# RWKV half of a hybrid layer: the score branch's output taken out of its own visit and put into the fourth level of the triangular inverse

## The reference

```python
p = x @ w_in
o_sb = stick_breaking_attention(q, k, v)      # 8 heads of 128
o_rw, _ = rwkv7_group(p[..., 3072:], ...)     # 16 heads of 64
h = concatenate([o_sb, o_rw], axis=-1) @ w_out

# score branch, for each head
z = einsum('qd,sd->qs', q, k) * d ** -0.5
log_a = z + lax.cumsum(where(mask, log_sigmoid(-z), 0), reverse=True)
o_sb = exp(where(mask, log_a, -inf)) @ v

# RWKV branch, for each head and token
S = S * w_t - (S @ kk_t) (kk_t * a_t)^T + v_t k_t^T
y_t = S @ r_t
```

## Time and profile before

| | |
|---|---|
| median of three runs | 3052.69 us (3048.38 to 3052.90) |
| the profiled execution, its own time | 3052.2 us |
| its span | 3050.5 us |
| PE busy | 2962.2 us, 97% |
| DVE busy | 1798.3 us, 59% |
| ACT busy | 1453.9 us, 48% |
| mean DMA rate | 161 GB/s |
| chain that ended last, PE's share | 91% |
| the seven narrow groups with a mixer, period | 59.5 us each (L512 at 85.50, 145.04, ... 442.69) |

### The profile page before, as it was taken

One profiled execution on the slowest core, in us unless ns is written; L12 is line 12 of the kernel. 1 busy time (PEld: TensorE's weight loads), 2 busy tenths in 40 slices (PEclk: granted clock), 3 DMA queues, 4 the chain that ended last, 5 costly groups with the idle time before them and its releaser, 6 DMA issues.

```text
span 3050.5 us, 55918 instructions
## 1 busy us (share of the span) xinstructions
PE 2962.2 (97%) x22084; PEld 2607.1 (85%) x22084; DVE 1798.3 (59%) x2375; ACT 1453.9 (48%) x2241; POOL 13.1 (0%) x28
## 2 busy tenths in 40 slices
PE   8999999999999999999999999999999999999997
PEld 8888887778888888889999997999977888888886
DVE  4655565575554555564666665566667545555555
ACT  4544544344343444434566664456654434444342
POOL 0000000000000000000000000000000000000000
PEclk9999999999999999999999999999999999999999
DMA  7333334455555555544334433544335555555553
GB/s 228 110 111 106 108 115 138 166 191 192 190 188 192 187 193 188 190 160 138 120 135 142 137 128 136 182 140 139 132 121 219 191 192 186 194 190 192 188 187 111
DMA packets 156999, 491.86 MB, mean 161 GB/s; under 512 B 15584, under 2 KB 50528, under 8 KB 155776
## 3 DMA queue, kind: packets, MB, share of 16 engines
q1 hardware_dynamic: 154032, 476.18, 45.9%
q0 software_dynamic: 2224, 11.69, 1.0%
q10 hardware_dynamic: 544, 1.05, 0.1%
HBM read 486.76 MB, written 2.10 MB: 160 GB/s over the span
## 4 chain that ended last, share of the span: by engine, by line
PE 91%; DVE 5%; ACT 2%; issue 1%; DMA 0%; ACTq 0%; DVEq 0%; SPq 0%
PE pp L420 45%; PE mp L420 11%; PE pp L404 8%; PE mp L404 8%; PE pp L406 4%; PE mp L406 4%; PE mp L810 1%; PE mp L774 1%; PE mp L758 1%; PE mp L750 1%; DVE wl L1356 1%; ACT wh L886 1%; PE mp L816 1%; PE mp L556 0%; PE mp L572 0%
## 5 line engine op out<-in xcount | busy, mean ns | idle before, releaser
L1356 DVE TENSOR_TENSOR wl<-raw,wh 128x1024 fp32r<-128x1024 f32 (+1 forms) x936 | 1101.3, 1184 | 853.3 <-ACT wh L886 850.3
L886 ACT CAST wh<-raw 128x1024 fp32r<-128x1024 f32 (+1 forms) x936 | 944.7, 1019 | 862.2 <-PE pp L420 287.4
L420 PE MATMUL pp<-aT,wh 128*128 128x256 f32 x4704 | 899.3, 291 | 6.0 <-DVE wl L1356 6.0
L420 PEld LDWEIGHTS pp<-aT,wh 128*128 128x128 f32 x4704 | 734.8, 192 | 21.4 <-issue 6.9
L420 PE MATMUL pp<-aT,wl 128*128 128x256 f32 x2352 | 666.7, 283 | 0.0
L420 PEld LDWEIGHTS pp<-aT,wl 128*128 128x128 f32 x2352 | 451.2, 192 | 0.0
L420 PE MATMUL pp<-wh,hTh 128*128 128x512 f32 x896 | 360.1, 402 | 7.9 <-DVE hTl L1610 6.0
L404 PE MATMUL pp<-aT,wh 128*128 128x512 f32 x1024 | 364.3, 400 | 0.8 <-issue 0.8
L404 PE MATMUL mp<-aT,wh 128*128 128x512 f32 x1024 | 360.0, 397 | 0.0
L420 PE MATMUL pp<-wh,hTl 128*128 128x512 f32 x896 | 350.8, 392 | 0.0
L420 PE MATMUL pp<-wl,hTh 128*128 128x512 f32 x896 | 350.3, 391 | 0.0
(11 more groups left out here) (301 smaller groups left out, 2674.1 us busy)
## 6 DMA issues: line engine op xcount, KB each, us to landing
raw<-in_w_dram SPq DMA_DIRECT2D x800, 512.0 KB, 3.3
raw<-in_w_dram SPq DMA_DIRECT2D x136, 384.0 KB, 3.5
ws<-in_ln_dram POOLq DMA_DIRECT2D x8, 1024.0 KB, 6.2
out_dram<-xres SPq DMA_DIRECT2D x8, 256.0 KB, 2.0
ws<-in_lora_dram POOLq DMA_DIRECT2D x8, 192.0 KB, 3.5
xres<-in_x_dram ACTq DMA_DIRECT2D x2, 512.0 KB, 6.1
xres<-in_x_dram SPq DMA_DIRECT2D x2, 512.0 KB, 7.0
ws<-in_c_dram POOLq DMA_DIRECT2D x1, 576.0 KB, 7.1
```

What stands on the lines that cost most here:

```text
L420: last = mm(o, lhs, rhs, start=opens and m == 0, stop=end and kk == 1 and m == 2, skip_group_check=True)
L886: nc.scalar.copy(wh[:, q % RING, :, 0:width], raw[:, q, :, 0:width]).then_inc(S("hi_ready"), 1)
L1356: tt(wl[:, q % RING, :, 0:width], raw[:, q, :, 0:width], f(wh[:, q % RING, :, 0:width]), ALU.subtract).then_inc(S("lo_ready"), 1)
```

## The change

`HOPS0` loses one visit: `(3, 3, 2, 2, 2)` becomes `(3, 3, 3, 3)`; the shares still sum to 32. Each generator loses visit 4. PE issues `sb_o` into `mb[1]` behind `dX` of level 4, waiting for `attn` and for the k and b tokens to have been copied; to that end ACT copies these one level earlier. ACT copies `sb_o` to `hTh` behind its copy of level 4, DVE makes `hTl` at level 5 in place of one piece of the token shift, and that piece goes behind the inverse. The wait for `sb_lo` moves from the Gram matrices to the product behind the inverse that writes `mb[1]` again (`WT`), and the wait there for the second `tok_ready` goes to `sb_o`.

```diff
-HOPS0 = (3, 3, 2, 2, 2) + 16 * (1,) + (0, 1, 0, 1, 0, 1, 1)
+HOPS0 = (3, 3, 3, 3) + 16 * (1,) + (0, 1, 0, 1, 0, 1, 1)
 # PE
-                pe.wait_ge(S("attn"), m1)
-                mm(mb[3][:, 0:T], vtk[:, 0, :], sba[:, 0:T], start=True, stop=False, skip_group_check=True)
-                mm(mb[3][:, P:T], vtk[:, 1, :], sba[:, T:384], start=False, stop=True,
-                   skip_group_check=True).then_inc(S("sb_o"), 1)
-                yield
                 pe.wait_ge(S("operands"), m1)
-                pe.wait_ge(S("sb_lo"), m1)
...
                     last.then_inc(S("dX"), 1)
+                    if lv == 4:
+                        pe.wait_ge(S("attn"), m1)
+                        pe.wait_ge(S("tok_ready"), 2 * m1)
+                        mm(mb[1][:, 0:T], vtk[:, 0, :], sba[:, 0:T], start=True, stop=False, skip_group_check=True)
+                        mm(mb[1][:, P:T], vtk[:, 1, :], sba[:, T:384], start=False, stop=True,
+                           skip_group_check=True).then_inc(S("sb_o"), 1)
                     yield
...
-                pe.wait_ge(S("tok_ready"), 2 * m1)
+                pe.wait_ge(S("sb_lo"), m1)
 # ACT
-                act.wait_ge(S("sb_o"), m1)
-                nc.scalar.copy(hTh[:, bass.ds(m * 2, 1), :], mb[3][:, 0:T].unsqueeze(1)).then_inc(S("sb_hi"), 1)
-                yield
...
-                    if lv == 2:
+                    if lv == 1:
                         st(nc.scalar.copy(BK[half(0), :, :], r2(mb[1][half(0), :], a=4)))
...
-                    if lv == 5:
+                    if lv == 4:
+                        act.wait_ge(S("sb_o"), m1)
+                        nc.scalar.copy(hTh[:, bass.ds(m * 2, 1), :], mb[1][:, 0:T].unsqueeze(1)).then_inc(S("sb_hi"), 1)
+                    elif lv == 5:
 # DVE
-                dve.wait_ge(S("sb_hi"), m1)
-                tt(hTl[:, bass.ds(m * 2, 1), :], mb[3][:, 0:T].unsqueeze(1), f(hTh[:, bass.ds(m * 2, 1), :]),
-                   ALU.subtract).then_inc(S("sb_lo"), 1)
-                yield
...
-                    if lv > 2:
+                    if lv == 5:
+                        dve.wait_ge(S("sb_hi"), m1)
+                        tt(hTl[:, bass.ds(m * 2, 1), :], mb[1][:, 0:T].unsqueeze(1), f(hTh[:, bass.ds(m * 2, 1), :]),
+                           ALU.subtract).then_inc(S("sb_lo"), 1)
+                    elif lv > 2:
                         next(pieces, None)
```

More of the change, by code:

```diff
@@ L997, in mix0 @@
                 for lv in range(1, 6):
-                    if lv == 2:
+                    if lv == 1:
                         st(nc.scalar.copy(BK[half(0), :, :], r2(mb[1][half(0), :], a=4)))
+                    elif lv == 2:
+                        st(nc.scalar.copy(BK[half(1), 1:4, :], r2(mb[1][half(1), 0:3 * P], a=3)))
                     elif lv == 3:
-                        st(nc.scalar.copy(BK[half(1), 1:4, :], r2(mb[1][half(1), 0:3 * P], a=3)))
-                    elif lv == 4:
                         nc.scalar.copy(BK[half(1), 0, :], mb[1][half(1), 3 * P:4 * P]).then_inc(S("tok_ready"), 1)
@@ L1569, in mix0 @@
                     yield
+                next(pieces, None)
                 next(pieces, None)
```

## The result

The changed kernel takes 3067.94 us (median of four runs, 3066.26 to 3070.03), the kernel before 3051.73 us (four runs, 3048.38 to 3052.90): a ratio of 1.0057 with a 95% interval of 1.0045 to 1.0069. It is slower by 16.2 us. Forecast were +17.2 us and 3069.9 us. Two of their launches had a lower mean granted clock than the 0.986 to 0.992 of all others: one of experiment 2 (3984.66 us at 0.681), which is left out of its numbers, and one of experiment 6 (3053.86 us at 0.941), which is kept.

A forecast was written before the change was run, and what follows sets the result against it. PE, busy 97% of the span, was taken as the bound, its waits set by a late DVE chain. 4.6 (`sb_o`) + 2.75 (eighth mixer) + 9.8 (clock) = 17.2 us gave 3069.9 us, range 3057 to 3075.

The forecast's parts named there:

- The same DVE stretch releases both waits: Narrow groups: one late DVE chain causes PE's waits before `sb_o` (1.17 us) and unit 5 (0.25); they become one 2.34 us stretch.
- `sb_o` at level 4, 0.66 us each: Seven narrow groups: `sb_o` is paid in PE's full stream at level 4, 7 x 0.66 = 4.6 us, bounds 3.5 to 6.4.
- The recorded lower bound of 0.5 us: `sb_o` at level 4: its lowest price per narrow group, if the two switches cost nothing.
- Eighth mixer, 2.76 us: Eighth mixer: `lcum` comes 2.76 us later, unit 8 directly behind it; PE idles some 2.65 us; bounds 2.6 to 2.9.
- The clock, seven of eight stretches at 1.4 us: Behind the new idle stretches PE's clock falls to 0.50 in seven of eight, 9.8 us in all, bounds 0 to 12.8.
- its strongest rival: New idle stretches: PE's clock stays up, so only 7.35 us is lost, 3060.0 us; chance 0.20.
- The sum: Whole kernel: 4.6 + 2.75 + 9.8 = 17.2 us slower, 3069.9 us, +0.56%.
- The waits go: Narrow groups: unit 5's split is on time, saving 10.0 us; 3042.7 us, or 3045.5 with the eighth mixer's loss; chance 0.05.
- No net effect: Levels 4 and 5: stretch only re-labelled, `sb_o` finds a pause of PE at level 4; 3053 to 3057 us; chance 0.07.
- more than forecast: Behind the stretches: low clock delays unit 5 through level 1, causing a second stretch, some 1 us per group; 3078 us; chance 0.06.

The follow-up runs named there:

- experiment 2: Changed kernel, but the eighth mixer gets its own table (3, 3, 2, 4), 14 halves ahead of `lcum` as before the change; 3063.76 us, ratio 1.0049.
- experiment 6: Kernel before, `sb_o` not moved, shares (3, 4, 2, 2, 1) in the narrow groups so unit 5's split comes early; 3047.64 us, ratio 0.9995.
- experiment 1: Kernel before with only `sb_o` moved to level 4; old table (3, 3, 2, 2, 2) and an empty fifth visit kept; 3064.46 us, ratio 1.0049.
- experiment 5: Changed kernel with shares (3, 4, 3, 2), putting unit 5's split ahead of DVE's long piece, and (3, 3, 2, 4) in the eighth mixer; 3037.18 us, ratio 0.9964.
- experiment 3: Kernel before, `sb_o` in its own visit, only the shares changed to (3, 3, 3, 1, 2) in all eight mixers; 3056.81 us, ratio 1.0022.
- experiment 4: Changed kernel with unused matmuls filling the new idle stretches, three per narrow group and four in the eighth mixer; 3060.58 us, ratio 1.0037.

## Why the prediction was right

- **"The same DVE stretch releases both waits".** Shown by experiment 1 (the move alone gives seven stretches of 2.35 us) and from the other side by experiment 5 (the split taken out of that stretch, the wait gone). Forecast 2.34 us, measured 2.33. In the fifth mixer, the one without a fall behind it, the Gram matrices start 6.76 us behind `lcum` (7.87 before) and 14.32 behind the scores (14.34 before), as forecast.
- **`sb_o` at level 4, 0.66 us each.** 0.65 us by the periods. No wait came at levels 4 and 5. The recorded lower bound of 0.5 us comes from no row: `lcum`'s first product has 384 columns, as many as `sb_o`'s two together, and takes 0.64 us of PE (144.98 to 145.62).
- **Eighth mixer, 2.76 us.** A stretch of 2.65 us, as forecast; experiments 2 and 3 show it to be the table's work and not the move's.
- **The clock, seven of eight stretches at 1.4 us.** Seven of eight fell, at 1.3 to 1.5 us in the narrow groups. This decided between the forecast and its strongest rival (3060.0). That it was seven is luck in part: the forecast had two rows with a fall, and behind the stretch of one of them, 2.68 us, the clock fell in only five of the ten profiles (last section). That a fall was likelier than not is borne out: 24 of the 28 narrow stretches of the changed kernel (two profiles) and of experiments 1 and 2. The rule of the Trainium skill ("TensorE: Matmul & The Clock Gate", section "HAM oscillation — how this bites in real kernels"), which warns of idle gaps of PE only from a greater length on, is not borne out as a bound below which they do no harm: gaps of 2.33 us were followed by the fall six times in seven, and experiment 4 fills most of each gap, changes nothing else, and the clock stays.
- **The sum.** The terms come to 17.4 us with the measured sizes, the median moved by 16.2. Between the two profiled executions it was 14.4, since the rest of the kernel is not equal in them: unit 5 of the first mixer already starts 1.0 us later, and from the restart behind the eighth mixer to the end of the span it is 2456.1 us in the profile before and 2451.9 in the one after. So the last 1 or 2 us of the agreement are chance.
- **The rivals.** *The waits go* needs the split 2.3 us earlier, which the changed kernel doesn't give; experiment 5 gives it, and there the waits do go, for the 10.0 us that this rival had counted. *No net effect* and *more than forecast* are out by the periods: no second stretch followed a fall.

## What to carry to other kernels

Before you take away a wait, ask what the engine would meet next. Two waits in a row can be two steps of one late chain, and the work between them was free; move that work away and its time comes back as idle time, here with a fall of TensorE's clock on top. Where one table places work on several engines, follow each placed item on each of them: a half more or less ahead of a visit puts another unit's preparation behind a long piece. And a gap that can't be closed can be worth filling, though closing it is worth more: experiment 4 is still 11 us slower than the kernel before, experiment 5 is 13 us faster.

## What was not expected of the hardware

- Length alone does not decide whether the clock falls. Three stretches recur in all ten profiles (nine kernels, the changed one twice). Behind the one of 1.75 to 1.77 us the clock fell in nine, not in experiment 5; behind the one of 2.68 us in five: before, after (twice), experiments 3 and 5; behind one of 3.36 or 3.37 us, ahead of the output projection, in eight, not in experiments 4 and 5. Windows right behind three of those without a fall, first 1.75 us in experiment 5, then 2.68 us in experiment 1, then 3.37 us in experiment 4:

```profile
1417.00:1421.00 4.00, 3.82 (x30) 3.61 (x31) 4.00 (x7) 3.43 (x4) 0.00 (x0) 1.00 0.38 133
...
607.60:611.00 3.40, 3.40 (x15) 2.80 (x16) 3.35 (x3) 1.67 (x3) 1.06 (x2) 1.00 0.59 226
...
494.20:498.00 3.80, 3.76 (x17) 3.12 (x18) 2.36 (x2) 2.84 (x4) 0.00 (x0) 1.00 0.07 10
```

  What else decides was not tried.
- The first MLP, from PE's last wait of 0.93 us ahead of it to the first transposes behind it, has no edit, and took 717.1 us in the profile before, 714.1 after and 718.6 in experiment 1. Its first 3.3, 2.9 and 5.7 us ran at a clock of 0.50, left over from longer waits of PE ahead of it. From there on, at 1.00, it is still not equal (before, after, experiment 1):

```profile
622.70:1336.49 713.79, 709.08 (x3594) 601.67 (x3593) 398.84 (x343) 300.05 (x295) 1.57 (x3) 1.00 0.56 193
...
641.00:1352.12 711.12, 705.96 (x3595) 600.12 (x3594) 399.07 (x344) 300.18 (x295) 1.56 (x3) 1.00 0.56 193
...
636.70:1349.49 712.79, 708.04 (x3587) 600.35 (x3585) 396.35 (x340) 299.54 (x294) 1.57 (x3) 1.00 0.58 193
```

  The mean of its 512-column matmuls into `pp` (L404) was 395 ns after and 398 in experiment 1. Such shifts of 2 to 4 us limit what a median says of a change of this size; the cause stays open.
